# Two transformer blocks in split fp32r: down panels split sooner, the last two down products together, high parts and convolution inputs moved

## The reference

```python
def swiglu(h, w_gu, w_down):            # ffn1, ffn2: width 2816
    g, u = jnp.split(h @ w_gu, 2, axis=-1)
    return (jax.nn.silu(g) * u) @ w_down
def _sq_relu_mlp(h, w1, w2):            # mlp1, mlp2: width 4096
    return jnp.square(jax.nn.relu(h @ w1)) @ w2
def sandwich(x, fn, g_pre, g_post, shift, scale, gate, res_w):
    h = modulate(rmsnorm(x, g_pre), shift, scale)
    y = rmsnorm(fn(h), g_post)
    return x + res_w * gate[:, None, :] * y
# first block: sandwich(ffn1), sandwich(mixer: chunked attention + RG-LRU), sandwich(ffn2)
# second block, two layers: mixer of four branches (differential and grouped attention over
# tokens and 256 context tokens, a Fourier branch, a gated convolution of 31 taps), then the MLP
# shift, scale, gate: silu(c) @ w + b, 9216 columns in the first block, 2 x 6144 in the second
# (there for two conditions: c of the tokens, c_ctx of the context)
```

## Time and profile before

| | |
|---|---|
| median of 3 runs | 4226.61 us (4221.52 to 4228.09) |
| profiled execution | 4226.4 us, span of its instructions 4224.5 us, mean granted clock 0.971 |
| TensorE busy | 3943.8 us (93%) |
| VectorE, ScalarE, GpSimd busy | 2207.9, 1367.0, 1349.9 us |
| where TensorE waits for a low part | 36.4 us, 20 times |

### The profile page before, as it was taken

The page is one execution under the profiler, slowest core; times in us unless marked ns, Lnnn a source line. Parts: engine busy times, 40 slices in busy tenths (PEclk is TensorE's granted clock), DMA queues, the critical chain, the costliest instruction groups (busy, mean ns, idle before and its releaser), DMA issues.

```text
span 4224.5 us, 51168 instructions
## 1 busy us (share of the span) xinstructions
PE 3943.8 (93%) x18864; PEld 3173.4 (75%) x18864; DVE 2207.9 (52%) x3379; ACT 1367.0 (32%) x1826; POOL 1349.9 (32%) x1012
## 2 busy tenths in 40 slices
PE   7999897989998889999999979999898998999999
PEld 6788685877776757857888768888684856777887
DVE  4667756135666352256832267777635256724334
ACT  3222644241223343253132331111334242334223
POOL 2444341433433201202343213332230403553443
PEclk8999999999999999999999989999999999999999
DMA  4454221223332101101111123333110201222222
GB/s 185 164 184 179 80 90 50 90 72 147 139 149 90 57 11 40 56 1 40 60 70 70 60 80 119 119 110 119 50 67 1 86 9 60 90 104 76 99 95 83
DMA packets 57220, 364.69 MB, mean 86 GB/s; under 512 B 5744, under 2 KB 12144, under 8 KB 13936
## 3 DMA queue, kind: packets, MB, share of 16 engines
q1 hardware_dynamic: 42064, 271.11, 18.2%
q10 hardware_dynamic: 15008, 91.49, 5.7%
HBM read 360.49 MB, written 2.10 MB: 86 GB/s over the span
## 4 chain that ended last, share of the span: by engine, by line
issue 66%; POOL 25%; PE 8%; POOLq 0%; DVE 0%; ACT 0%; DVEq 0%; ACTq 0%
POOL b_wlo L579 25%; PE ps L1719 3%; PE ps L1721 3%; PE ps L1720 3%; POOLq L593 0%; DVE b_y L1218 0%; POOLq L595 0%; DVE b_x L1222 0%; DVE b_y L1271 0%; PE ps L1804 0%; ACT b_whi L620 0%; PE ps L1791 0%; ACT b_xout L685 0%; DVE b_small L1220 0%; POOLq L579 0%
## 5 line engine op out<-in xcount | busy, mean ns | idle before, releaser
L579 POOL TENSOR_TENSOR b_wlo<-b_raw,b_whi 128x512 fp32r<-128x512 f32 x1008 | 1349.7, 1371 | 2854.1 <-ACT b_whi L620 2854.1
L1719 PE MATMUL ps<-b_hhi,b_whi 128*128 128x512 f32 x3032 | 1122.9, 370 | 26.4 <-POOL b_wlo L579 8.4
L1720 PE MATMUL ps<-b_hlo,b_whi 128*128 128x512 f32 x3032 | 1111.2, 366 | 0.0
L1721 PE MATMUL ps<-b_hhi,b_wlo 128*128 128x512 f32 x3032 | 1110.6, 366 | 0.0
L620 ACT ACTIVATE b_whi<-b_raw 128x2048 fp32r<-128x2048 f32 x252 | 481.2, 1910 | 762.5 <-PE ps L1721 745.8
L1719 PEld LDWEIGHTS ps<-b_hhi,b_whi 128*128 128x128 f32 x3032 | 574.7, 190 | 126.4 <-issue 24.1
L1721 PEld LDWEIGHTS ps<-b_hhi,b_wlo 128*128 128x128 f32 x3032 | 574.5, 189 | 94.1
L1720 PEld LDWEIGHTS ps<-b_hlo,b_whi 128*128 128x128 f32 x3032 | 575.0, 190 | 92.9 <-issue 1.9
L1166 DVE SCALAR_TENSOR_TENSOR b_macc<-b_mraw,b_csil,b_macc 128x256 f32<-128x256 f32 x868 | 504.0, 636 | 7.0
L1271 DVE TENSOR_TENSOR b_y<-ps,b_y 128x512 f32<-128x512 f32 x496 | 335.9, 689 | 283.8 <-PE ps L1721 283.7
L1719 PE MATMUL ps<-b_whi,b_dhi 128*128 128x512 f32 x992 | 403.9, 407 | 52.2 <-POOL b_wlo L579 27.9
(11 more groups left out here) (301 smaller groups left out, 4825.7 us busy)
## 6 DMA issues: line engine op xcount, KB each, us to landing
b_raw<-panels SPq DMA_DIRECT2D x252, 1024.0 KB, 4.8
b_mraw<-mod_panels ACTq DMA_DIRECT2D x78, 1024.0 KB, 6.7
b_y<-mod_panels ACTq DMA_DIRECT2D x3, 1024.0 KB, 16.0
b_xin<-xT SPq DMA_DIRECT2D x1, 2048.0 KB, 25.6
b_mraw<-mod_panels SPq DMA_DIRECT2D x2, 1024.0 KB, 18.9
b_rope<-rope ACTq DMA_DIRECT2D x4, 512.0 KB, 3.7
outT<-b_xout SPq DMA_DIRECT2D x4, 512.0 KB, 3.6
b_mod<-mod_panels ACTq DMA_DIRECT2D x1, 1024.0 KB, 20.9
```

The costliest lines, as they stand in the source:

```text
L579: ins = pool.tensor_tensor(wlo[:, s, c], raw[:, s, c], whi[:, s, c].bitcast(F32), ALU.subtract)
L1719: pe.matmul(out, a[0], b[0], start=first, stop=False)
L1720: pe.matmul(out, a[0], b[1], start=False, stop=False)
L1721: return pe.matmul(out, a[1], b[0], start=False, stop=last)
```

## The change

1. ScalarE's `units` splits the gated down panel p + 2 as soon as the first up panel is used, ahead of taking that panel's product. In the last chunk it splits the last down panel ahead of the second half chunk's product.
2. The modulation panels are dealt out differently: ffn1 (2, 3, 3), then 3 a round, 2 in the last; ffn2 1, 3, six rounds of 2, then 3 and 1; mlp1 1, twelve rounds of 2, then 3 and 0. The last one or two rounds stand outside the loop (`rest`).
3. The down products of the last two chunks are made together (`last_downs`): three half groups of chunk C - 2, the last sums, the gate row, then the panel of chunk C - 1 is waited for and each group accumulates both chunks in its bank. VectorE adds each group once, in `finish`. The next stage's first panel is split by the norm, behind the last tile's post root. The zero panel is no longer split.
4. In `norm_low` VectorE copies `hhi` from `hf`, for odd k at 512 tokens and for all k but 0 and 4 at 768.
5. n3's two context tiles are normalised between the others, not ahead of them.
6. The second and third convolution input stand behind 10 and 20 taps (mix2), 7 and 14 (mix3), before 11 and 23.

```diff
@@ -233,9 +233,10 @@
-        self.lead, self.half, self.trips = mods
+        self.lead, self.half, self.trips, self.tail = mods
         self.loop0 = 1 + len(self.lead)
         self.rest = range(self.loop0 + 2 * self.trips, self.C)
+        assert len(self.tail) == len(self.rest) >= 1
         self.per_trip = 2 * (self.UP + 1)
@@ -249,6 +250,11 @@
+
+    def rest_mods(self, c):
+
+        n = c - self.rest[0]
+        return self.mod0 + sum(self.lead) + 2 * self.trips * self.half + sum(self.tail[:n]), self.tail[n]
@@ -465,10 +471,10 @@
     first = {**{n: 10 ** 6 for n in ("mix1", "ffn2", "mix2", "mlp1", "mix3", "mlp2")}, **first}
-    MLPS = {"ffn1": Mlp("ffn1", True, L, first["ffn1"], 8, ((2, 2), 3, 4)),
-            "ffn2": Mlp("ffn2", True, L, first["ffn2"], 36, ((), 2, 5)),
-            "mlp1": Mlp("mlp1", False, TT, first["mlp1"], 56, ((), 2, 7)),
-            "mlp2": Mlp("mlp2", False, L, first["mlp2"], 84, ((), 0, 7))}
+    MLPS = {"ffn1": Mlp("ffn1", True, L, first["ffn1"], 8, ((2, 3, 3), 3, 3, (2,))),
+            "ffn2": Mlp("ffn2", True, L, first["ffn2"], 36, ((1, 3), 2, 3, (3, 1))),
+            "mlp1": Mlp("mlp1", False, TT, first["mlp1"], 56, ((1,), 2, 6, (3, 0))),
+            "mlp2": Mlp("mlp2", False, L, first["mlp2"], 84, ((), 0, 7, (0,)))}
@@ -523,17 +529,23 @@
         early = [t for t in TILES(pre[0] if pre else 0) if post and t >= post[0] // P]
-        out = [("pre", t) for t in early]
+        out = []
         last = (post or pre)[0] // P
...
                 out.append(("pre", n - 1))
+            if n < len(early):
+                out.append(("pre", early[n]))
         return out
...
+
+    def hi_by_vector(T, k):
+
+        return k % 2 == 1 if T <= L else k % 4 != 0
@@ -600,7 +612,7 @@
         for st in [s for s in ORDER if s in NORMS and NORMS[s][0]]:
-            upto = next_panel(st) + 1 if st in NEXT else n_panels
+            upto = next_panel(st) + 1 if st in NEXT else MLPS["mlp2"].p0 + 2 * MLPS["mlp2"].C
             low_parts(done, upto)
@@ -656,6 +668,8 @@
                     root(st, what, t, yt[:, t, :])
+                    if t == last and pre:
+                        split(next_panel(st))
                 else:
@@ -674,7 +688,8 @@
                     bank = turn_banks(st)[k % len(turn_banks(st))][0]
-                    for dst, kind in ((hhi[:, k, :], "h_hi"), (hf[:, k % 3, :], "hf")):
+                    whole = (hf[:, k % 3, :], "hf")
+                    for dst, kind in ((whole,) if hi_by_vector(T, k) else ((hhi[:, k, :], "h_hi"), whole)):
                         for g, (a, b) in groups(T):
@@ -695,10 +710,14 @@
                         mod_load(mods[0] + v, i, 2 * m.half)
-                    if m.gated or n == 0:
-                        split(p + n + 1, i, m.per_trip)
+                    if n == 0:
+                        split(p + 1, i, m.per_trip)
                     if m.gated or n == 1:
                         act.wait_ge(panel_used, lin(p + (n if m.gated else 0) + 1, m.per_trip, i))
+                        if n == 0:
+                            split(p + 2, i, m.per_trip)
+                        elif c == m.C - 1:
+                            split(p + m.UP + 1)
                     else:
@@ -724,9 +743,9 @@
             for c in m.rest:
-                units(c, m.panel(c))
-                split(m.panel(c) + m.UP + 1)
-            split(m.p0 + m.UP * m.C + m.C)
+                units(c, m.panel(c), mods=m.rest_mods(c))
+                if c < m.C - 1:
+                    split(m.panel(c) + m.UP + 1)
             gate_rows(AFTER[st], (0, 1, 2, 3))
@@ -1233,6 +1252,8 @@
                     dve.wait_ge(*at("hf", (st, k, groups(T)[-1][0])))
+                    if hi_by_vector(T, k):
+                        chain(dve.tensor_copy(hhi[:, k, 0:T], hf[:, k % 3, 0:T]))
                     dve.tensor_tensor(hlo[:, k, 0:T], hf[:, k % 3, 0:T],
@@ -1265,7 +1286,7 @@
                 else:
-                    dve.wait_ge(panel_used, lin(down_panel(m, c) + 1, m.per_trip, i))
+                    dve.wait_ge(panel_used, lin(down_panel(m, c if c < m.C - 2 else m.C - 1) + 1, m.per_trip, i))
                 dve.wait_ge(*at("added", ("start", st), lin(O * c + o + 1, 2 * O, i)))
@@ -1281,14 +1302,15 @@
             for c in m.rest:
-                units(c)
-                for o in range(O):
-                    add(c - 1, o)
+                units(c, mods=m.rest_mods(c))
+                if c < m.C - 1:
+                    for o in range(O):
+                        add(c - 1, o)
             prepare(AFTER[st])
             def finish(t):
-                add(m.C - 1, 2 * t)
-                add(m.C - 1, 2 * t + 1)
+                add(m.C - 2, 2 * t)
+                add(m.C - 2, 2 * t + 1)
                 C.name("y", (AFTER[st], t), "added", C.count["added"])
@@ -1640,14 +1662,15 @@
             keep_lo("g", 4, cl, ch, lambda k: aq[:, k, 0:T])
+            in_1, in_2 = (10, 20) if T > L else (7, 14)
             conv_input(0)
-            taps(0, 11)
+            taps(0, in_1)
             conv_input(1)
-            taps(11, 23)
+            taps(in_1, in_2)
             conv_input(2)
...
             in_g0, in_g1, in_dft = (46, 74, 87) if T > L else (38, 60, 77)
-            taps(23, in_g0)
+            taps(in_2, in_g0)
             merge("g", 0, pg, lambda t: tap(in_g0 + t))
@@ -1877,16 +1900,44 @@
                         ins.then_inc(*up("down"))
-                    if c == m.C - 1 and o == 1:
-                        gate_rows(AFTER[st], (0, 1, 2, 3))
                 ins.then_inc(panel_used, 1)
-            first_ups()
+            def last_downs():
+
+                p, c = m.panel(m.C - 1) + m.UP, m.C - 2
+                def part(o, n):
+
+                    tok, half = slice(o // 2 * P, (o // 2 + 1) * P), o % 2
+                    if n == 0:
+                        prior = O * (c + 1) + o - 3 if o >= 3 else O * c + max(q for q in range(O) if q % 3 == o)
+                        pe.wait_ge(*at("added", ("start", st), prior + 1))
+                    for k in range(2):
+                        ins = tri(ps[:, 4 + o % 3, :], (dhi[:, (c + n) % 2, k, tok], dlo[:, (c + n) % 2, k, tok]),
+                                  wtile(p + n, 2, D, k, half * 512, 512), n == k == 0, n == k == 1)
+                    if o == O - 1:
+                        ins.then_inc(panel_used, 1)
+                    elif n == 1:
+                        ins.then_inc(*up("down"))
+
+                pe.wait_ge(lo_ready, p + 1)
+                pe.wait_ge(*at("hid_lo", ("start", st), 2 * c + 2))
+                for o in range(3):
+                    part(o, 0)
+                sums(m.rest_mods(m.C - 1))
+                gate_rows(AFTER[st], (0, 1, 2, 3))
+                pe.wait_ge(lo_ready, p + 2)
+                pe.wait_ge(*at("hid_lo", ("start", st), 2 * c + 4))
+                for o in range(O):
+                    if o >= 3:
+                        part(o, 0)
+                    part(o, 1)
+
...
+            first_ups()
             for n in range(len(m.lead)):
@@ -1899,8 +1950,10 @@
                 ups(c, m.panel(c))
-                down(c - 1, m.panel(c) + m.UP)
-            down(m.C - 1, m.p0 + (m.UP + 1) * m.C - 1)
+                if c < m.C - 1:
+                    down(c - 1, m.panel(c) + m.UP)
+                    sums(m.rest_mods(c))
+            last_downs()
```

## The result

The changed kernel takes 4186.16 us (median of 4, 4179.30 to 4188.27), the one before 4226.62 (median of 4). The ratio is 0.9904, with an interval of 0.9886 to 0.9921: faster, by 40 us where the prediction had 32, and inside its range of 4172 to 4212. The profiled execution took 4188.27 us with a span of 4186.5, 38 shorter than that of before.

A forecast was written before the change was run, and what follows sets the result against it. TensorE was taken as the bound, busy 3943.8 of 4224.5 us, so only its idle stretches and slow matmuls counted. Terms 36.5 - 0.5 - 33.5 + 8.0 + 3.7 + 6.5 + 10.4 = 31.1 us gave 4195, range 4172 to 4212.

The forecast's parts named there:

- The early split: Splitting the gated down panel sooner removes low-part waits in ffn1's first round, ffn2's first round and loop: 36.5 us gained.
- mlp1's first round: One modulation panel instead of two ahead of the adds shortens TensorE's 7.78 us wait: 8.0 us gained, bounds 6 and 10.
- ffn1's other rounds: The early split delays the third modulation panel's transfer, mostly made up on VectorE: 0.5 us lost, bounds 0 and 9.
- The third panel: Three-panel rounds stall TensorE for late adds: 21.4 us lost in ffn2's two, 12.1 in mlp1's one, 33.5 together.
- rival (b): Early low part lands on VectorE's modulation sums in every gated round, adds come late: costs 60 us, 4255; chance 0.06.
- part 5: Convolution inputs placed behind fewer taps in mix3 and mix2 shorten TensorE's waits: 10.4 us gained, bounds 8 and 12.
- part 3: Last two down products made together at the four MLP ends: 3.7 us gained in sum, bounds -4 and 13.
- High parts by VectorE: In the norms, VectorE's copies shorten TensorE's waits for low parts: 6.5 us gained, 3 at 768 wide, 3.5 at 512.
- (a): The third modulation panel does not stall TensorE, its transfer in time or sums undisturbed: 4161 us; chance 0.08.
- (c): Gate column and GpSimd's collision cost 3 us more in each of four stages, 768-wide copy gains nothing: 4210; chance 0.14.
- (d): The early split doesn't help because raw data or GpSimd is late, all its gaps staying: 4231 us; chance 0.04.

The follow-up runs named there:

- e1: Changed kernel with the gated down panel split where it was before, behind the first half chunk's product; 4202.3 us.
- e2: Changed kernel with the modulation panels dealt as before (two a round in ffn2 and mlp1, none with three; ffn1 2, 2, then 3); 4170.3 us.
- e6: Changed kernel with the next stage's first panel split behind the root of the last tile's pre part instead of its post part; 4185.4 us.
- e4: Changed kernel with the last two down products apart again and the next stage's first panel split at the MLP's end; 4173.9 us.
- e5: Changed kernel with two of its three three-panel rounds evened out (ffn2 ending 2, 2; mlp1 ending 2, 1); 4157.7 us.
- e7: Changed kernel with all high parts of the norms' tails made by ScalarE again, as before; 4198.5 us.
- e3: Changed kernel with the third modulation panel's transfer issued ahead of the first half chunk's activation instead of behind its product; 4171.8 us.
- e9: Changed kernel with the edits of e3 and e5 together, last two down products still joined; 4160.3 us.
- e11: e9's kernel with the first round's modulation transfers issued ahead of the first two half chunks' activations; 4155.0 us.
- e10: e9's kernel with the last two down products apart, run beside it on the same chip; 4153.3 us.
- e12: e11's kernel with ffn2's modulation panels even, two in each of the ten rounds; 4152.3 us.

## Why the prediction held, and where it was off

The forecast sum is 31.1 us; the medians lie 40.5 apart, the profiled spans 38.0. Over the table, ffn2's two three-panel rounds bring 9 us more than forecast; all other departures, of up to 3.2 us either way, come to -2.5 together. That these cancel is luck, and two of them, the start and the wait in ffn1, are chance.

**The early split.** Right in ffn1's first round and in ffn2's loop (5.1 for 4.9; 16.7 in six rounds for 15.6; undone in e1, 5.0 and 15.7). In ffn2's first round the number, 11.2 for 10.9, was right by another cause. The forecast had the low part ready some 3 us early by the split alone; e2, with the split and two panels, still waits 4.53 for it, and keeps 4.9 of the 11.2. The single panel, priced in mlp1's first round alone, brings 9.9 without the split (e1). The sum was not touched, since the kernel has both edits and they remove the same wait.

**ffn1's other rounds** (-0.5, bounds 0 and 9 lost) gave -3.7. It is one wait, in the fourth round. ScalarE issues the third transfer there at 203.00, and VectorE's row shows it landed at 210.42:

```profile
203.00 0.34 ACTq L640 DMA_DIRECT2D b_mraw<-mod_panels  x1
```

```profile
210.42 0.36 DVE L1182 TENSOR_SCALAR b_macc<-b_mraw,b_csil 128x256 f32<-128x256 f32 x1 [5.69 <-DMA b_mraw<-mod_panels]
```

7.4 us, where the earlier trace rows has 4.88. The wait is in the profiles of the changed kernel and of e6 (2.41, transfer 7.4) and, at 1.0, of e2 (6.0); it is absent in those of e1, e4, e5 and e7, which have the same rounds there and transfers of 5.0 to 5.1. So it is chance, worth up to 4 us, and in e3, e9 and e11, where the third transfer is sooner, it is not seen. Why the one transfer took longer no row shows.

**The third panel** was the step that was mis-sized. In mlp1 it cost 13.2 where 12.1 were reckoned. In ffn2 it cost 6.5 and 5.9 (a round without it gains 2.8, these lost 3.8 and 3.1), 12.4 in place of 21.4; against e2, which has two panels there, it is 7.4 and 6.8. The prediction put the two sums' end at S+19.6, since the early low part would hold VectorE in the second sum as the ordinary one does in the first. The rows of chunk 2, with S at 988.45, show VectorE undisturbed:

```profile
988.97 9.76 DVE L1185 SCALAR_TENSOR_TENSOR b_macc<-b_mraw,b_csil,b_macc 128x256 f32<-128x256 f32 x14
...
999.18 5.62 DVE L1185 SCALAR_TENSOR_TENSOR b_macc<-b_mraw,b_csil,b_macc 128x256 f32<-128x256 f32 x14
...
1006.10 1.66 DVE L1281 TENSOR_TENSOR b_dlo<-b_tmp,b_dhi 128x512 fp32r<-128x512 f32 x1 [0.70 <-ACT b_dhi L734]
...
1010.52 0.61 DVE L1182 TENSOR_SCALAR b_macc<-b_mraw,b_csil 128x256 f32<-128x256 f32 x2 [2.76 <-DMA b_mraw<-mod_panels]
```

```profile
1001.70 8.46 POOL L591 TENSOR_TENSOR b_wlo<-b_raw,b_whi 128x512 fp32r<-128x512 f32 x4 [6.02 <-ACT b_whi L632]
```

```profile
1005.44 0.33 ACTq L640 DMA_DIRECT2D b_mraw<-mod_panels  x1
```

The first sum takes 9.76 us beside GpSimd, as in the earlier trace rows. The second takes 5.62, as if alone, and it is GpSimd that waits: 8.46 us for four instructions. So the sums end at S+16.4, the transfer is issued at S+17.0 and not S+20.5, lands (5.1 us) at S+22.1, and the stall is 4.64: the forecast's 8.1 less 3.5. The same error is why rival (b), at 4255, had no foundation: the collision falls on the engine that has time.

**mlp1's first round, both convolution inputs.** Right, with 8.2 for 8.0 (e2, with two panels there, gives 7.6 back) and 11.8 for 10.4; in mix2 the wait is now 2.40. No run undoes part 5 (item 6 of the change), so its cause rests on the waits alone, 1.50 for 8.40 and 2.40 for 4.16.

**The joined products.** The prediction gave the whole of part 3 +3.7, of which +5.9 in ffn2. The 5.45 us wait of the earlier trace rows is gone in e4 and e10 too (e4 gains some 6 us at ffn2's end), so the joining did not remove it. What these keep is the new order of the context tiles. Before, the adds stood behind the tiles' norm steps on VectorE:

```profile
1353.71 0.75 DVE L1229 TENSOR_SCALAR b_y<-b_x,b_small 128x1024 f32<-128x1024 f32 x1
1354.38 1.88 DVE L1271 TENSOR_TENSOR b_y<-ps,b_y 128x512 f32<-128x512 f32 x3
```

No run undoes that order by itself. Without that wait and its 2.5 of slow clock, the prediction's own terms for joining make -4.3; the runs say -2 to -7, ffn2 doing better and mlp2 worse than reckoned. GpSimd's collision at the norm's steps was right in kind: 4.54 for 2.91 of wait, and a step of 2.09 us where 1.28 is usual. The gate column's waits were forecast as 0.6, 2.0, 2.6 and 1.5 us and are 1.39, 1.40, 3.67 and 2.18. mlp2's end was priced at nothing, because the chain of tiles was taken to end as before; it ends 2.1 us later.

**High parts by VectorE.** Right and undersized: 8.7 by place, 12 by the medians, for 6.5. The copy, which the trace of before did not have, is in the list of groups:

```profile
L1256 DVE CAST b_hhi<-b_hf 128x768 fp32r<-128x768 f32 x18 | 10.1, 560 | 24.2 <-ACT b_hf L694 24.2
L1256 DVE CAST b_hhi<-b_hf 128x512 fp32r<-128x512 f32 x16 | 6.8, 427 | 2.1 <-ACT b_hf L694 2.1
```

0.560 us at 768 wide, close to the 0.6 taken. The Trainium skill (VectorE: DVE Perf Modes, The perf-mode tier table) has such a copy at twice a subtraction's rate; beside the subtractions of 0.96 (768 wide) and 0.69 (512) these are 1.7 and 1.6 times. For the 256 columns between the two sizes the copy takes 0.133 us more and the subtraction 0.266, which is the twofold rate; the rest, 0.16 us, is alike in both.

**The rivals.** (a), no stall at three panels, is refuted by the waits of 4.64, 3.80 and 10.00, though one of its grounds, sums that run beside GpSimd undisturbed, holds for the second sum. (b) is refuted by the rows above. (c), sour ends, is not borne out: joining costs 2 to 7 us, where the forecast's own terms make 4.3 and the rival 12 more, and the copies gained. (d), a useless early split, is refuted by e1.

**Slips in the working.** Four slow products at 1.6 are 6.4 and not 6.2; S+34.3 less S+26.3 is 8.0 and not 8.1, twice. Together they move the sum by 0.4 us. The copy at a subtraction's rate would by its own terms be worth 1.0 and not 0.5. The second row is the fourteenth down product, not the twelfth; the ones between wait 0.56 as well.

**Left open.** A kernel of e12 with its last down products apart, by the pair e9 and e10 some us quicker, wasn't tried. Nor is it known why GpSimd alternates with VectorE at one panel and stands still at the next.

## What to carry to other kernels

When work is dealt out anew over rounds, look at the chain inside the fullest round: a third item needs the slot of the first, a transfer of 5 us and its own sum, and it stalled the product that followed, while the same item in a round at the end that had room cost next to nothing. Undo each edit of a change by itself, even when the whole is a gain: of this one's parts, the new deal cost 16 us and the joined products a few, hidden under over 60 us of gains. And where two edits remove the same wait, the sum of single prices is not what either is worth.

## What the runs showed of the hardware

VectorE and GpSimd, when both read operands from SBUF, share by whole instructions, but not always evenly. While GpSimd makes the low part of ffn2's second up panel they alternate: VectorE's steps go from 0.47 to 1.5 us, GpSimd's take 1.47. At the down panel, split early, GpSimd's first instruction stood for as long as VectorE's steps followed one another: 3.5 to 3.8 us in each of ffn2's two-panel rounds, 4.3 in chunk 2, and in e12, where VectorE's stream ran on for 6.7 us, 7.2 us for one instruction of usually 1.3 (the row has all four). In e2 it was 9.1, and it began within the same sum in which the two had alternated 4 us before, so the difference goes by the panel and not by the sum. The row of e12:

```profile
960.60 11.36 POOL L591 TENSOR_TENSOR b_wlo<-b_raw,b_whi 128x512 fp32r<-128x512 f32 x4 [3.48 <-ACT b_whi L632]
```

None of this length is in the trace of before or of e1. This is what makes two panels dear in ffn2's first round (4.53 us of wait in e2, 2.65 in e12). The Trainium skill (SBUF — State Buffer, Who interferes with whom) tells of an exclusive lock, held for a whole instruction while the other engine is blocked. The alternating steps agree with it. That the two take turns, as the prediction put it, it doesn't say, and the standing still, over 15 instructions of VectorE in a row (7.2 us), is no turn-taking.

Slow clock follows the waits, as before: after the 4.64 us wait the first matmul takes 0.79 us and the next six 0.63, where 0.40 is usual, and the mean granted clock of the whole execution went from 0.971 to 0.974, in e12 to 0.980.
